# Two more column blocks of an input projection by seven half-size products, a new VectorE order, and a new order of the last stores

## The reference, cut to what matters

```
u = rmsnorm(x) @ w_in                      # 1024 -> 4368 columns, split into
qa, ka, va, qb, kb, vb, g_low, r_b, g_a, g_b
oa = sliding-window attention(qa, ka, va)
ob = gated linear attention(qb * 0.125, kb, vb, decay from g_low)   # "GLA"
h  = x + (sigmoid(g_a) * (oa @ w_a) + sigmoid(g_b) * (rmsnorm(ob) * silu(r_b)) @ w_b) @ w_o
y  = h + top-4-of-32 experts(rmsnorm(h))   # each 1024 -> 2048 -> 1024, 12 MB of weights
```

## Time and profile before

| | |
|---|---|
| three runs, median | 1184.53 us (1183.4 to 1185.93) |
| the profiled execution, its own time | 1185.38 us |
| its span, first to last instruction | 1183.3 us |
| busy: TensorE, VectorE, ScalarE | 1149.6, 366.7, 177.3 us |
| moved by DMA | 440.03 MB, mean 372 GB/s |
| granted TensorE clock, mean | 0.992 |

### The profile page before, as it was taken

The page is one execution under the profiler, slowest core; times in us unless marked ns, Lnnn a source line. Parts: engine busy times, 40 slices in busy tenths (PEclk is TensorE's granted clock), DMA queues, the critical chain, the costliest instruction groups (busy, mean ns, idle before and its releaser), DMA issues.

```text
span 1183.3 us, 14232 instructions
## 1 busy us (share of the span) xinstructions
PE 1149.6 (97%) x6178; PEld 569.1 (48%) x6178; DVE 366.7 (31%) x758; ACT 177.3 (15%) x327; POOL 28.9 (2%) x54
## 2 busy tenths in 40 slices
PE   9999999999999999999999999999999989899997
PEld 8679997545434343434344343434343434343433
DVE  3637876323312122222223221212121212121222
ACT  2225233012101110101011010101010101010111
POOL 4120000000000000000000000000000000000000
PEclk9999999999999999999999999999999999999999
DMA  9443358958999999999999999999999999999996
GB/s 304 145 119 109 93 172 279 423 204 332 422 429 434 427 437 428 429 436 427 434 432 426 434 430 428 433 434 430 429 430 436 426 431 434 426 433 423 426 426 225
DMA packets 45969, 440.03 MB, mean 372 GB/s; under 512 B 3790, under 2 KB 21552, under 8 KB 29760
## 3 DMA queue, kind: packets, MB, share of 16 engines
q1 hardware_dynamic: 43760, 434.19, 88.2%
q0 software_dynamic: 1904, 4.10, 1.2%
q10 hardware_dynamic: 240, 0.79, 0.2%
HBM read 436.38 MB, written 3.67 MB: 372 GB/s over the span
## 4 chain that ended last, share of the span: by engine, by line
PE 73%; DMA 24%; issue 1%; ACT 1%; DVE 1%; ACTq 0%; DVEq 0%
PE ps L1259 25%; DMA ring<-in_w 24%; PE ps L1323 14%; PE ps L798 6%; PE ps L1345 4%; PE ps L1124 3%; PE ps L1025 3%; PE ps L1047 2%; PE ps L765 2%; PE ps L755 1%; PE ps L732 1%; PE ps L1274 1%; PE ps L1132 1%; ACT xnT L1704 1%; PE ps L1286 1%
## 5 line engine op out<-in xcount | busy, mean ns | idle before, releaser
L1259 PE MATMUL ps<-ring,hnT 128*64 128x512 f32 x2032 | 450.4, 600 | 10.6 <-DMA ring<-in_w 10.6
L1259 PEld LDWEIGHTS ps<-ring,hnT 128*64 128x64 f32 x2032 | 144.0, 138 | 300.7 <-issue 281.7
L1323 PE MATMUL ps<-ring,xnT 128*64 128x512 f32 x992 | 220.7, 597 | 9.0 <-DMA ring<-in_w 8.9
L2238 DVE TENSOR_TENSOR xnT<-ps,b1T 128x512 f32<-128x512 f32 x32 | 22.1, 692 | 425.3 <-PE ps L1274 425.3
L1323 PEld LDWEIGHTS ps<-ring,xnT 128*64 128x64 f32 x992 | 74.7, 138 | 150.5 <-issue 149.6
L1691 ACT COPY hnT<-ps 128x1024 f32<-128x1024 f32 x32 | 32.4, 1012 | 504.2 <-PE ps L1259 504.2
L2259 DVE TENSOR_TENSOR acc<-acc,ps 128x1024 f32<-128x1024 f32 x30 | 36.6, 1219 | 222.3 <-PE ps L1345 206.1
L1345 PE MATMUL ps<-xnT,cst 128*128 128x512 f32 (+1 forms) x180 | 76.1, 619 | 1.5
L1124 PE MATMUL ps<-cst,region 128*128 128x128 f32 x512 | 63.5, 283 | 0.7 <-issue 0.7
L1124 PEld LDWEIGHTS ps<-cst,region 128*128 128x128 f32 x512 | 60.1, 196 | 2.8 <-issue 0.9
L1703 ACT COPY xnT<-ps 64x512 f32<-64x512 f32 x31 | 17.9, 579 | 247.9 <-PE ps L1323 247.9
(11 more groups left out here) (314 smaller groups left out, 837.5 us busy)
## 6 DMA issues: line engine op xcount, KB each, us to landing
ring<-in_w SPq DMA_DIRECT2D x74, 4096.0 KB, 36.1
ring<-in_w SPq DMA_DIRECT2D x31, 2048.0 KB, 36.5
ring<-in_w SPq DMA_DIRECT2D x20, 1024.0 KB, 9.4
ring<-in_w_in SPq DMA_DIRECT2D x17, 1024.0 KB, 5.5
ring<-in_w_o SPq DMA_DIRECT2D x2, 2048.0 KB, 12.0
ring<-in_w SPq DMA_DIRECT2D x8, 512.0 KB, 23.5
ring<-in_w_b SPq DMA_DIRECT2D x1, 2048.0 KB, 11.5
ring<-in_w_a SPq DMA_DIRECT2D x4, 512.0 KB, 6.0
```

The lines of the kernel that those rows point to most:

```text
L1259: mm = pe.matmul(ps[o:o + 64, bank + q // 2, into].rearrange("p (j x) -> p j x", x=4), stationary, columns[:, q], start=(at == 0), stop=(a ...
L1323: mm = pe.matmul(ps[64 * c:64 * c + 64, 6, :], hT[:, which, order_of(f), :], ring[:, slot, D * (f % 2) + 512 * c:D * (f % 2) + 512 * c + 512],
L2238: dve.tensor_tensor(glu, ps[:, 2, :].rearrange("p (f t) -> p f t", f=KF), wide(b1T[:, bass.ds(e, 1), 0, :].rearrange("p a f -> p (a f)").u ...
```

## The change

- `PLAIN_UNITS` goes from 7 to 5: the units of `qb` and `kb` join the half-size products, as the first two of now twelve. Their tiles (four of sixteen) are gone from `TILE_ORDER`; `glow` and `vb` move up behind the last `q` tile. The scale 0.125 of `qb` goes into ScalarE's copies of unit 0 (`activation(..., Copy, scale=...)` for all group copies).
- The products start with the tile `vb 2`, four tiles earlier. The attention steps are dealt out anew over the twelve units on TensorE, ScalarE and VectorE; `gla_operands` now also waits for the first two units' outputs.
- `sum_x` is done right behind the normed activations, ahead of the copy of the norm vectors (line 1800).
- The loads of units follow: five are issued at once, the rest behind what frees their slots.
- At the end, `combine_end` is split by prompt tile. The second left half comes behind `down_end(1, 1)`, the sample tile comes ahead of the right halves; VectorE's additions and SyncE's stores follow the same order.

```diff
-W_UNITS = [C_K, C_Q, C_Q + UNIT, C_QB, C_KB, C_VB, C_VB + UNIT] + [C_RB + UNIT * i for i in range(2)] \
+W_UNITS = [C_K, C_Q, C_Q + UNIT, C_VB, C_VB + UNIT, C_QB, C_KB] + [C_RB + UNIT * i for i in range(2)] \
-PLAIN_UNITS = 7
+PLAIN_UNITS = 5
-PLAIN_SLOTS = [9, 8, 11, 10, 6, 7, 19]
-FAST_SLOTS, SUM_SLOTS, TURNED_SLOT = [8, 6, 7], [9, 10], 11
+PLAIN_SLOTS = [9, 6, 7, 8, 10]
+FAST_SLOTS, SUM_SLOTS, TURNED_SLOT = [6, 7, 8], [9, 10], 11
-    + [("qb", j) for j in range(2)] + [("kb", j) for j in range(2)] + [("glow", 0)] \
+    + [("glow", 0)] \
...
@@ TensorE
             beside = {
                 8: [cache_keys],
-                10: [lambda: scores(0), new_keys],
-                13: [lambda: turn_probs(0), lambda: scores(1)],
-                14: [lambda: attend(0), gate_logits],
-                15: [lambda: turn_probs(1), lambda: scores(2)],
+                9: [lambda: scores(0), new_keys],
+                10: [gate_logits],
+                11: [lambda: turn_probs(0), lambda: scores(1)],
             }
...
-                7: [lambda: decays("decays_p", [0, 1])],
-                8: [lambda: turn_probs(4), lambda: decays("decays_s", [2])],
-                9: [lambda: attend(4)],
+                11: [lambda: turn_probs(4)],
+                12: [lambda: attend(4), lambda: decays("decays_p", [0, 1])],
+                13: [lambda: decays("decays_s", [2])],
...
-                combine_end(p, 0)
+                combine_end(p, 0, 0)
                 down_end(1, 1, b)
+                combine_end(p, 0, 1)
                 pe.wait_ge(y_copied, 2 * p + 2)
-                combine_end(p, 1)
                 combine_sample()
+                for t in range(2):
+                    combine_end(p, 1, t)
@@ ScalarE
-                    out = nc.scalar.copy(products(u, i, n), ps[:, (group + 1) % 3, HALF_T * part:HALF_T * (part + n)])
+                    out = nc.scalar.activation(products(u, i, n), ps[:, (group + len(TILE_ORDER)) % 3, HALF_T * part:HALF_T * (part + n)],
+                                             ACT.Copy, scale=1.0 if u else SCALE)
@@ VectorE
                                          ).then_inc(xnT_ready, 1)
+            dve.wait_ge(xnT_ready, KD)
+            dve.tensor_tensor(sum_x(3), block_x(2, 2), block_x(1, 2), ALU.subtract)
+            link(dve.tensor_tensor(sum_x(1), block_x(1, 2), block_x(1, 1), ALU.subtract))
+            link(dve.tensor_tensor(sum_x(2), block_x(2, 2), sum_x(1), ALU.subtract))
+            dve.tensor_tensor(sum_x(4), block_x(2, 1), sum_x(2), ALU.subtract).then_inc(halves_ready, 1)
             dve.wait_ge(n_ready, use(N_USES, "vectors"))
             dve.tensor_copy(cols[:, 8:21], ps[:, NB, 0:13]).then_inc(n_freed, 1)
...
             def gla_operands():
                 dve.wait_ge(exps_ready, 1)
+                dve.wait_ge(out_ready, 2)
...
@@ SyncE
+            sp.wait_ge(comb_added, 3 * HALF + 1)
             for half in range(2):
                 store_half(2, half)
+            for t in range(2):
+                sp.wait_ge(comb_added, 3 * HALF + t + 2)
+                store_half(t, 1)
```

More of the change, by code:

```diff
@@ L93, in unit_done @@
 def unit_done(m):
[L95 removed]
+    last = [("va", 2), ("q", 3), ("q", 3), ("vb", 2), ("vb", 2)]
     return tiles_done(*last[m])
@@ L430, in load_unit @@
                              ).then_inc(unit_in[m % UNIT_SEMS], 16)
-            for m in range(PLAIN_UNITS - 1):
+            for m in range(PLAIN_UNITS):
                 load_unit(m)
@@ L435, in _ @@
                     sp.dma_start(cst[:, 2 * P:NCONST], consts[:, 2 * P:NCONST]).then_inc(consts_in, 16)
[L436 to L439, removed]
+            for u, old in enumerate((1, 2, 3)):
+                sp.wait_ge(pj_ready, unit_done(old))
                 load_unit(PLAIN_UNITS + u)
@@ L758, in project @@
                     return
[L759 to L761 removed]
+                need_unit(0)
                 for k in range(KD):
[L763 to L765 removed]
+                    pe.wait_ge(xnT_ready, k + 1)
+                    mm = pe.matmul(ps[:, bank, 0:T], unit(0)[:, k, 0:P], xnT[:, k, :],
                                    start=(k == 0), stop=(k == KD - 1))
@@ L797, in product @@
                 for k in range(4):
-                    mm = pe.matmul(ps[:, (group + 1) % 3, HALF_T * part:HALF_T * part + HALF_T], w[:, k, :], x[:, k, :],
+                    mm = pe.matmul(ps[:, (group + len(TILE_ORDER)) % 3, HALF_T * part:HALF_T * part + HALF_T], w[:, k, :], x[:, k, :],
                                    start=(k == 0), stop=(k == 3), skip_group_check=True)
@@ L1288, in down_end, with combine_end @@
                 mm.then_inc(w2_used, 1)
[L1290 to L1294, removed]
+            def combine_end(p, c, t):
+                t0, r = TILES[t]
+                pe.matmul(ps[:, (0, XB)[c] + t, :], gpickT[:, t0:t0 + r], y_sb[:, 512 * c:512 * c + 512],
+                          start=True, stop=True).then_inc(comb_done if c else half_done, 1)
             def combine_sample():
@@ L2040, in _ @@
             fast_sums(3)
+            softmax_max(4)
+            weight_sums(6)
+            attended(3)
+            softmax_norm(4)
+            fast_sums(4)
+            gla_operands()
+            weight_sums(7)
+            attended(4)
+            mask_decays_prompt()
+            fast_sums(5)
             mask_decays_sample()
-            attended(4)
-            weight_sums(6)
-            fast_sums(4)
+            weight_sums(8)
             mask_keys(0)
+            fast_sums(6)
             step_states(0)
             mask_keys(1)
-            weight_sums(7)
+            weight_sums(9)
             step_states(1)
             mask_keys(2)
-            fast_sums(5)
+            fast_sums(7)
             step_states(2)
-            weight_sums(8)
-            fast_sums(6)
+            weight_sums(10)
+            fast_sums(8)
             step_states(3)
-            weight_sums(9)
-            fast_sums(7)
+            weight_sums(11)
+            fast_sums(9)
             dve.wait_ge(gates_ready, 2)
-            fast_sums(8)
+            fast_sums(10)
             link(dve.tensor_tensor(rbT[:, :, :], rbT[:, :, :], rsT[:, :, :], ALU.mult))
-            fast_sums(9)
+            fast_sums(11)
             def merge_a(m):
```

132 lines of the change are left out of this document (59 added, 73 removed).

## The result

| | before | after |
|---|---|---|
| median of the runs, us | 1185.34 (20 runs, 1183.40 to 1187.73) | 1183.24 (20 runs, 1181.35 to 1185.93) |
| profiled execution: own time, span, us | 1185.38, 1183.3 | 1185.93, 1183.7 |

The ratio after to before is 0.9982, 95% interval 0.9975 to 0.9988: 2.1 us less. The prediction was 4.0 us less and 1180.5 us, with a range of 1179.0 to 1183.2; the median lies at its upper edge, 0.04 us outside. Measured beside the new kernel, the median of before is 0.8 us above the one of three runs that the prediction started from, so -4.0 would have been 1181.3; the gain came out at half of what was forecast. The two profiled executions don't show even that: their spans are 1183.3 and 1183.7. Two things in them have to be taken apart before they can be compared, a drop of TensorE's clock and the last store.

A forecast was written before the change was run, and what follows sets the result against it. TensorE was taken to bound the kernel up to 282 us, the expert weight stream to 1156, then the last expert's end. Front -1.3 and end -2.7 sum to -4.0 us: 1184.53 - 4.0 = 1180.5 us, range 1179.0 to 1183.2.

The forecast's parts named there:

- TensorE's net and the group copy: Ahead of the first branch: half-size products save TensorE 1.64 us, the last group's two copies cost 0.33 us.
- Activation sums, `gla_operands`, scaled copies, loads: In front: VectorE's added or moved work, ScalarE's scaled group copies and the reordered loads delay nothing, 0 us.
- cover at the decays: VectorE finishes `gla_operands` ahead of TensorE's decays; about 4 us of cover was to stay.
- Rival E: Slower: VectorE reaches the end of `gla_operands` late; 11 us late gives 1187.5 us. Chance 0.06.
- B: Only the end's gain: TensorE gives the front's 1.3 us back to waits for VectorE or ScalarE; 1181.8 us. Chance 0.14.
- The front's gain gets through the stream: Expert weight stream, 282 to 1156 us: TensorE earlier by d us starts the stream and ends the kernel d us earlier.
- The end, 0.9 of earlier addition: Kernel's end: the new order finishes the last addition 0.9 us earlier, part of the end's 2.7 us gain.
- The end, the rest, 1.8: Kernel's end: the remainder of the 2.7 us gain, from a last store of 128 rows landing after 2.1 us.
- a last store of near 4 us: Sign in the profile after, at the kernel's end, that would show the prediction wrong.
- rival C: Kernel's end: the last store is as slow as the slow one before, end gain 1.4 us; 1181.8 us. Chance 0.12.

The follow-up runs named there:

- e7: Changed kernel with the products that combine the sample tile done four times over, adding TensorE work behind the last weights; 1184.24 us, ratio to before 0.9990.
- e11: Changed front with the old order of the end, and the sample's two stores issued by ScalarE; 1182.66 us, ratio to before 0.9985.
- e3: Kernel before with each qb and kb tile done twice, 17.24 us more of TensorE in front; 1202.14 us, ratio to before 1.0137.
- e2: Changed kernel with the old end put back, so the new front alone; 1182.94 us, ratio to before 0.9977.
- e1: Kernel before with only the new order of the last combine, additions and stores; 1185.03 us, ratio to before 0.9996.
- e4: Changed kernel run once more, unaltered, beside the others on one chip; 1183.11 us, ratio to before 0.9979.
- e5: Changed kernel without the skipped blocks of further expert passes on all engines and their token-count reads; 1181.06 us, ratio to before 0.9960.
- e9: Changed kernel without the skipped blocks of further expert passes on TensorE and VectorE alone; 1180.57 us, ratio to before 0.9958.
- e6: Changed kernel with the last two prompt stores (right halves) issued by ScalarE instead of SyncE; 1181.16 us, ratio to before 0.9963.
- e10: Changed kernel with the sample's two stores issued by ScalarE instead of SyncE; 1180.69 us, ratio to before 0.9969.
- e8: Changed kernel without the sample tile's two stores at the end, output unwritten, a probe alone; 1180.67 us, ratio to before 0.9961.

## Why the prediction was half right

- **TensorE's net and the group copy, -1.64 + 0.33.** Right in kind, too small: -1.86. The first branch waits for 0.81 us in place of 0.47, as forecast (+0.34). The products' time rose from the 74.9 to the 90.3 us that their pieces sum up to, 15.4 for 15.6. What I didn't foresee is that the two `vb` tiles took 6.91 us each, not 7.10 (0.38 together). -17.24 + 15.41 + 0.34 - 0.38 = -1.87.
- **Activation sums, `gla_operands`, scaled copies, loads: 0.** Right. The first columns' copy at line 1800 is 2.15 us behind the start of `va`, as before (2.14). It was close: without a drop of the clock 0.15 us of idle time is left before it (e7, e11), as the 0.18 of the prediction said. The wait of line 760 is 1.1 us as before; cover at the decays 3.5 us for about 4; none of the eight table loads is on the group copies' line 1506, and no load of a unit stopped TensorE. Rival E never came near, and B fell.
- **The front's gain gets through the stream.** Right: e3 passes 16.7 of 17.24 us, and e2's time is that of the whole gain. The reading behind it was off in one point: the stream of weights doesn't end at 1156, since the DMA engines are busy for 0.69 of the time from 1164 to 1168. The sum doesn't use it.
- **The end, 0.9 of earlier addition.** Right in the traces: 0.82 to 0.88 in after, e1 and e4.
- **The end, the rest, 1.8.** This is the step that failed: "the rest is that the last store is one of 128 rows and not the second of two", taken to land after 2.1 us. It landed after 5.2 us in after, 4.1 in e4 and 4.4 in e1, and the stretch behind the last addition, 4.9 us before, was 6.1, 4.7 and 4.9 in place of 3.0. So of the 1.8 us nothing came. The prediction had named a last store of near 4 us as the sign that it was wrong. The 2.1 came from four stores of which none was last, the 3.9 from the one that was the earlier trace rows, and I laid the difference to what they carried. In its place stand instruction packets that are moved for TensorE and VectorE at that moment: one of 16 KB takes 0.9 us or more of a DMA engine while packets of the last store are waiting, and without the blocks that bring them the last store lands after 2.5 and 2.6 us (e5, e9). That the blocks cause the delay is shown by removing them; that the store's packets stand behind an instruction packet on the same DMA engine is inferred from the order in time. In the new order 512 KB of prompt stores follow directly on the sample's, and part of it is still to be moved when the packets come (from 1180 to 1181 the profile of after shows 49 packets of stores beside the 16 KB one).

So rival C, with 0.12, described what happened, a last store as slow as the slow one before, but not why; and the 0.5 us by which its 1.4 exceeds the 0.9 of the addition is hardly seen in the stretches behind (4.9 us before, 4.9 in e1, 4.7 in e4). The rule of the Trainium skill that stood beside the prediction's end (DMA: Bandwidth & Descriptors, "Latency and other measured facts": a fixed cost of about 2 us) agrees with the quickest landing, 2.1 us; it doesn't have the further 2 to 3 us of the last store in after, e1 and e4. With 0.9 in place of 2.7 the sum is -1.87 - 0.87 = -2.7 us, and the runs gave -2.1 (-1.4 to -3.0) and, e4, -2.4. That the total came to half of the forecast and not less is in part luck: the front brought 0.55 us more than its sum. A gain of the forecast's size is to be had: e6 keeps all of the computation and takes 1181.16 us, 0.37% less than before (0.24 to 0.49), where the changed kernel has 0.18% (0.12 to 0.25). e10, at 0.31%, can't be told from it.

## What to carry over

Before costing a store at the end by its landing, ask which store is last in the trace and what else the DMA engines move then: a landing time depends on what is moved beside it, and not only on the tile. Look at the small queues in the last 10 us; code that is skipped isn't free if it is fetched there. And where two profiles of nearly one front differ by a microsecond, compare the granted clock in short stretches and count between two events behind the drop before reading a gain or a loss into it.

## What the runs showed of the hardware

- TensorE's clock falls to the 1.2 GHz level once early in most executions. Of 14 profiles eleven have one early drop, nine at 12 to 16 us in the first tile (6.0 to 6.2 us for 4.55) and two at 270 to 277 us (3.65 for 2.02), and e7, e8 and e11 have none. Before the drop at 270, TensorE had been busy nearly without a break since 86 us and then idle for 0.7 of the 8 us from 258 on the earlier trace rows, and for 0.9 of the 6 us from 270 to 276. After has the same 0.9 us of idle time there and no drop, so what TensorE did doesn't tell the two apart; the code up to the first tile is the same in before and e3, and only e3 has the drop there. Each costs about 1.7 us.
- 16 KB instruction packets took 0.88 to 0.96 us of one DMA engine in the last 5 us of before and after. The longest near the end is in e2, 1.8 us from 1178 on (11.1% of 16 engines in 1 us). With the blocks that bring them gone, the last store lands after 2.5 us, 1.6 sooner than in e4.
- The issue of the sample's two stores on SyncE took 1.17 us before, but 1.76 in the profile of after and 1.33 in e4, where an instruction packet runs at 1175 to 1176, and 1.16 to 1.17 in e5 and e9, which have none. e6 has 1.75 with a packet that starts between 1174 and 1174.5. But e1 has 1.17 too, with a packet that starts just ahead, so the link is not shown. A slow issue holds what is queued behind it: in after the last store was issued 0.5 us behind its addition, in e7 1.4.
